# Two layers and a third part of a network on one core: three programs with barriers between them written as one

## The reference, cut to what matters

```python
for l in range(2):                                   # the two layers
    h = rms_norm(x, g_mix_pre);  u = h @ w_in        # 1024 -> 3200
    mix = concat(chunk_attention, conv_module, retention) @ w_out
    x = x + rms_norm(mix, g_mix_post)
    h = rms_norm(x, g_mlp_pre)
    f = square(relu(h @ w_up)) @ w_down              # 1024 -> 4096 -> 1024
    x = x + rms_norm(f, g_mlp_post)
# the third part
x = x + 0.5 * swiglu_ffn(rmsnorm(x, ffn1_norm))      # 1024 -> 2 x 2816 -> 1024
u = rmsnorm(x, mix_norm);  proj = u @ w_in_2
x = x + (gated sum of ssm, dilated attention, memory attention) @ w_out_2
x = x + 0.5 * swiglu_ffn(rmsnorm(x, ffn2_norm))
return rmsnorm(x, final_norm)
```

## Time and profile before

| | us |
|---|---|
| median of 3 runs | 2854.04 |
| lowest and highest | 2852.43, 2858.58 |
| the profiled execution | 2853.72 |
| its span | 2851.9 |
| PE busy | 2710.3 (95%) |
| DVE busy | 1291.4 (45%) |
| ACT busy | 1015.0 (36%) |

### The profile page before, as it was taken

How to read it: one execution, slowest core, us unless ns; L and a number is a source line. 1 busy time by engine, 2 the same in 40 slices (tenths; PEclk the granted TensorE clock), 3 DMA queues, 4 the chain that set the end, 5 groups by cost and what they waited for, 6 DMA issues and landing times. The chain is left out here.

```text
span 2851.9 us, 31899 instructions
## 1 busy us (share of the span) xinstructions
PE 2710.3 (95%) x12330; PEld 2122.2 (74%) x12330; DVE 1291.4 (45%) x1666; ACT 1015.0 (36%) x1433; POOL 287.8 (10%) x276
## 2 busy tenths in 40 slices
PE   7999899999799989999989999999999998899998
PEld 5875688887587568888768888777777666688886
DVE  4754442342574444233343333478773446333322
ACT  3333332232333333233333333433235453334322
POOL 0000000001000000000100000067540230000000
PEclk9999999999899989999999999999999999999999
DMA  3310122322231012322122322412131024122222
GB/s 123 126 53 30 59 82 95 104 88 74 72 122 45 30 59 88 103 89 103 59 82 96 103 92 91 168 60 74 53 132 52 30 75 162 61 101 90 94 91 80
DMA packets 41443, 241.88 MB, mean 85 GB/s; under 512 B 5232, under 2 KB 5744, under 8 KB 18416
## 3 DMA queue, kind: packets, MB, share of 16 engines
q1 hardware_dynamic: 41056, 239.25, 24.4%
q0 software_dynamic: 272, 1.05, 0.1%
HBM read 231.90 MB, written 8.39 MB: 84 GB/s over the span
## 5 line engine op out<-in xcount | busy, mean ns | idle before, releaser
L353 DVE TENSOR_TENSOR w_lo<-w_raw,w_hi 128x2048 fp32r<-128x2048 f32 (+3 forms) x219 | 464.2, 2120 | 850.4 <-ACT w_hi L344 850.2
L384 PE MATMUL gemm<-h_hi,w_hi 128*128 128x512 f32 x1936 | 777.7, 402 | 47.9 <-DVE h_lo L538 44.0
L384 PE MATMUL gemm<-h_hi,w_lo 128*128 128x512 f32 x1936 | 760.5, 393 | 0.0
L384 PE MATMUL gemm<-h_lo,w_hi 128*128 128x512 f32 x1936 | 760.5, 393 | 0.0
L344 ACT ACTIVATE w_hi<-w_raw 128x2048 fp32r<-128x2048 f32 (+3 forms) x219 | 383.5, 1751 | 257.5 <-PE gemm L384 254.3
L384 PEld LDWEIGHTS gemm<-h_hi,w_hi 128*128 128x128 f32 x1936 | 367.0, 190 | 139.0 <-issue 46.1
L384 PEld LDWEIGHTS gemm<-h_hi,w_lo 128*128 128x128 f32 x1936 | 367.2, 190 | 78.2
L384 PEld LDWEIGHTS gemm<-h_lo,w_hi 128*128 128x128 f32 x1936 | 368.1, 190 | 71.8 <-issue 1.7
L384 PE MATMUL gemm<-f_hi,w_hi 128*128 128x512 f32 x512 | 199.4, 389 | 0.0
L384 PE MATMUL gemm<-f_hi,w_lo 128*128 128x512 f32 x512 | 199.4, 389 | 0.0
L384 PE MATMUL gemm<-f_lo,w_hi 128*128 128x512 f32 x512 | 199.4, 389 | 0.0
(11 more groups left out here) (370 smaller groups left out, 3614.4 us busy)
## 6 DMA issues: line engine op xcount, KB each, us to landing
w_raw<-in_w SPq DMA_DIRECT2D x171, 1024.0 KB, 4.8
w_raw<-in_w SPq DMA_DIRECT2D x16, 768.0 KB, 4.2
w_raw<-in_w SPq DMA_DIRECT2D x16, 640.0 KB, 3.8
w_raw<-in_w SPq DMA_DIRECT2D x18, 512.0 KB, 3.7
bias_t<-in_att_bias SPq DMA_DIRECT2D x2, 1536.0 KB, 9.2
decay_t<-in_c_decay SPq DMA_DIRECT2D x2, 1536.0 KB, 8.2
x_sb<-in_x SPq DMA_DIRECT2D x4, 512.0 KB, 5.4
x_kept<-x_sb SPq DMA_DIRECT2D x1, 2048.0 KB, 11.0
```

Source lines behind the costliest of these rows:

```text
L353: dve.tensor_tensor(w_lo[:, b.slot, 0:size], w_raw[:, b.slot, 0:size], w_hi[:, b.slot, 0:size].bitcast(F32), ALU.subtract).then_inc(S["w_r ...
L384: mm = pe.matmul(dst, lhs, rhs, start=b.first and k == 0 and j == 0, stop=b.last and k == b.kt - 1 and j == 2)
```

## The change

The three blocks become one `nc.Block`. The layer's bodies are functions of the layer's number (`layer_tensor(pe, lay)` and so on), called twice in Python, so the outer loop is gone and the layer stands in the program twice. The semaphores are never cleared: a wait in layer `lay` adds what earlier layers have counted (`cnt`), and the norms are numbered through (`N0`). The pieces of all parts are numbered in one list. `load_next`, `round_next`, `rest_next`, `head_start`, `clear_counts` and the transfers of `first_gain` are gone; the gains of both layers and of the third part are loaded at the start. A block behind a border is now handled like every other, two blocks ahead.

```diff
-def number(pieces, tok_tiles=None):
+def number(*parts):
+    pieces = []
+    for part in parts:
+        for i, b in enumerate(part):
+            b.i = i
+            pieces.append(b)
...
-    plan1 = layer_pieces()
-    plan2, AT2 = third_pieces()
+    third_part, AT2 = third_pieces()
+    plan = number(*(layer_pieces() for _ in range(DEPTH)), third_part)
...
-        def round_block(act, plan, n, t=ONCE, whole=False):
-            if isinstance(t.n(n), int) and t.n(n) >= len(plan):
-                return
+        def piece_of(n, t):
+            if isinstance(t.i, int):
+                n, t = t.n(n), ONCE
+            return (plan[n], t) if n < len(plan) else (None, t)
+        def round_block(act, n, t=ONCE):
+            b, t = piece_of(n, t)
+            if b is None:
+                return
...
-        def clear_counts():
-            for s in S.values():
-                nc.gpsimd.sem_clear(s)
-            nc.all_engine_barrier()
...
-                norm_inverse(dve, 1)
-                for q in range(2):
-                    rest_next(dve, q)
-        clear_counts()
-        with nc.Fori(0, DEPTH) as layer:
-            with nc.Block() as block:
+            for n in range(2):
+                rest_block(dve, n)
...
                     norm_rooted(act, 3)
-                    round_next(act, 0, plan1)
                     norm_squares(act, 4, x_sb, sq_f, wait=(S["x_done"], KD))
                     norm_rooted(act, 4)
-                    round_next(act, 1, plan1)
...
                     post_norm_dve(dve, 3, gains["mlp_post"], KD)
-                    rest_next(dve, 0, n1)
-                    norm_inverse(dve, 4)
-                    rest_next(dve, 1, n1)
-            clear_counts()
...
-                head_start(dve)
-                pre_norm_dve(dve, 0, 0, first_gain)
+            pre_norm_dve(dve, N0 + 0, J0 + 0, gains["mix_pre"])
...
+        with nc.Block() as block:
+            @block.vector
+            def _(dve):
+                begin_vector(dve)
+                for lay in range(DEPTH):
+                    layer_vector(dve, lay, step)
+                third_vector(dve, step)
```

More of the change, by code:

```diff
@@ L214, in third_pieces @@
     ffn("ffn2")
-    tok_tiles = [MEMT if b.kind == "tok" and b.src == "w_kv" else TOKT for b in out]
-    return number(out, tok_tiles), start
+    return out, start
 def build(nc, ins, outs):
     A = ins
-    plan1 = layer_pieces()
-    plan2, AT2 = third_pieces()
+    third_part, AT2 = third_pieces()
+    plan = number(*(layer_pieces() for _ in range(DEPTH)), third_part)
+    n1 = (len(plan) - len(third_part)) // DEPTH
+    plan2 = plan[DEPTH * n1:]
     with ExitStack() as ctx:
@@ new lines, in begin_tensor, with begin_scalar, begin_vector @@
+        def begin_tensor(pe):
+            pe.wait_ge(consts_in, 32)
+            norm_total(pe, 1, out_sb)
+            pe.wait_ge(more_consts_in, 32)
+        def begin_scalar(act):
+            for k in range(0, KD, 2):
+                act.wait_ge(x_in[k // 2], 16)
+                norm_squares(act, 1, x_sb, out_sb, tiles=(k, k + 1))
+            act.wait_ge(eps_made, 2)
+            norm_rooted(act, 1)
+            for n in range(2):
+                round_block(act, n)
+        def begin_vector(dve):
+            dve.memset(eps_c[:], EPS).then_inc(eps_made, 1)
+            dve.memset(quarter[:], np.pi / 2).then_inc(eps_made, 1)
+            for n in range(2):
+                rest_block(dve, n)
@@ new lines, in layer_gpsimd @@
+        def layer_gpsimd(pool, lay):
+            cnt = counts(lay)
+            N0 = 1 + 4 * lay
+            pool.wait_ge(S["conv_inv"], cnt("conv_inv", 2))
+            for q in range(2):
+                tile = out_sb[:, 3 + q, :]
+                pool.tensor_tensor(tile, tile, conv_rs, ALU.mult).then_inc(S["ln_done"], 1)
+            pool.wait_ge(S["ln_done"], cnt("ln_done", 2))
+            pool.wait_ge(S["rg_gate"], cnt("rg_gate", PAIRS))
+            for j in range(1, PAIRS + 1):
+                tile = out_sb[:, 4 + j, :]
+                pool.wait_ge(S["ln_sq_s"], cnt("ln_sq_s", 2 + j))
+                pool.tensor_tensor(tile, tile, rg[:, j - 1, :], ALU.mult).then_inc(S["ret_gated"], 1)
+            squares_added(pool, N0 + 1, cnt("sq_added", 0), sq_f)
+            squares_added(pool, N0 + 3, cnt("sq_added", KD - 3), sq_f)
@@ L1250, in build @@
+            post_norm_dve(dve, N0 + 3, gains["mlp_post"], KD)
         g_hi = at("g_hi", [P, F2T, SEQ], F32R, FZ)
@@ L1346, in slot_of @@
             half, left = divmod(m + 1, b.tiles // 2)
-            return slot_at.get((b.n - first_q, half - 1)) if left == 0 else None
+            return slot_at.get((b.i - first_q, half - 1)) if left == 0 else None
         def residues(g, i):
@@ L1460, in _ @@
+                third_sync(sp)
+            @block.tensor
+            def _(pe):
+                begin_tensor(pe)
+                for lay in range(DEPTH):
+                    layer_tensor(pe, lay)
+                third_tensor(pe)
             @block.gpsimd
             def _(pool):
-                pool.wait_ge(S["units"], plan2[AT2["ffn1_down"]].u0)
-                pool.dma_start(mem_sb[:], A["mem"].rearrange("(k p) t -> p k t", p=P)).then_inc(S["mem_in"], 16)
-                squares_added(pool, 2, 0, x2_sq)
@@ L1751, in _ @@
+                for lay in range(DEPTH):
+                    layer_gpsimd(pool, lay)
+                third_gpsimd(pool)
             @block.scalar
             def _(act):
-                def evacuate(b, dst, func=ACT.Copy, scale=1.0, width=SEQ, m0=0):
-                    for m in range(b.tiles):
-                        act.wait_ge(S["units"], b.u0 + (m + 1 if b.kind == "feat" else m // 2 * 2 + 2))
-                        act.activation(dst(m), tile_of(b, m, width), func, scale=scale).then_inc(S["g_free"], 1)
@@ L2019, in _ @@
-                for b in plan2[AT2["w_out2"]:AT2["ffn2_up"]]:
-                    k = 2 * (b.n - AT2["w_out2"])
-                    if k:
-                        norm_squares(act, 3, x_sb, mix_sq, wait=(S["x2_done"], KD), tiles=(k - 2, k - 1))
-                    evacuate(b, lambda m: part[:, k + m, :])
-                    round_block(act, plan2, b.n + 2)
-                norm_squares(act, 3, x_sb, mix_sq, wait=(S["x2_done"], KD), tiles=(KD - 2, KD - 1))
-                norm_rooted(act, 3)
@@ L2027, in _ @@
-                split_hi(act, 3, 3, out_sb, S["normed"], 3 * KD)
-                ffn("ffn2", F2T)
-                norm_squares(act, 4, x_sb, out_sb, wait=(S["x2_done"], 2 * KD), tiles=(KD - 2, KD - 1))
-                norm_rooted(act, 4)
+                begin_scalar(act)
+                for lay in range(DEPTH):
+                    layer_scalar(act, lay)
+                third_scalar(act)
             @block.vector
```

2857 lines of the change are left out of this document (1415 added, 1442 removed).

## The result

The changed kernel takes 2840.04 us, the median of five runs (2839.23 to 2840.88), against 2854.04 for the kernel before in the same comparison: a ratio of 0.9948 (95% interval 0.9934 to 0.9963). The direction and the changed places came out as forecast; 4.5 us were won where the sum had nothing.

The account below looks back on a forecast made before the run. TensorE, busy 95% of the span, was taken as the bound, with gains only where it stands still. Gains of 2.9 us at the start, 4.0 and 1.2 at the borders made 8.1: 2845.9 us, range 2841.5 to 2850.5.

Parts of the forecast that it names:

- Start: Program start: first scaling at 26.36 us instead of 29.28, 2.9 us won, with the spread at the lower clock, 2.08 us.
- First border: Between the two layers: the next scaling comes 3.5 to 4.4 us earlier than at 734.11, taken as 4.0.
- The model place: Behind `w_out2` in the third part, already in the new order: 13.17 us from summing's start to scaling, assumed for both borders.
- Second border: Between second layer and third part: the scaling comes 0.8 to 1.6 us earlier than at 1438.36, taken as 1.2.
- Point (1): The layer's second copy in the program: instruction fetch could cost 3.8 us once or twice; taken as zero.
- Point (2): Clock level in the layers' norm spreads: either layer can gain or lose 1.8 us, taken as 2 us both ways.
- The rivals: Three alternative outcomes for the whole kernel: 2834.2 us (4 in 100), 2849.7 us (22 in 100), 2859.7 us (3 in 100).
- The first: At the borders the splits don't hold the norm back: 19.8 us gained, 2834.2 us; 4 in 100.
- The slower one: Clock stays down through each border's last norm: 6.9 us lost per border, 2859.7 us; 3 in 100.
- The range: Whole kernel: 2841.5 to 2850.5 us, including 2 us for the clock to either side; 71 in 100 for the forecast.

Follow-up runs that it names:

- late_splits: The changed kernel with each border's second rounding and split moved behind the post-norm's root and sums; 2829.45 us.
- unrolled_before: The kernel before with its loop over the two layers written out, barriers and clearing kept; 2846.93 us.
- experiment 10: The changed kernel with each border's second split behind the post-norm and the first norm's inversion ahead of the start's splits; 2826.87 us.
- idle_2: The changed kernel with two extra sums on DVE between spread and scaling at the first border alone; 2848.03 us.

## Why the prediction was wrong

- *Start*: forecast 2.9 us, came 2.85, with the spread at 2.07 us as taken (the 2.08 of the earlier trace rows). Right.
- *First border*: forecast 4.0 (3.5 to 4.4), came 4.37. The model place gave 13.17 us, measured 13.13; the stretch behind, 15.63, was nearer to the border's own 15.51 than to the 16.42 that I also averaged in. Right, and late_splits shows that the rounding and split in the norm's way make the 13.13 us out of 6.98.
- *Second border*: forecast 1.2 (0.8 to 1.6), came 1.65, just over the upper end, for the same reason: 13.13 + 15.56.
- *Point (1) of "What no row shows"*, the second copy at zero: right, as far as unrolled_before shows it.
- *Point (2)*, the failed step, a term of the sum that was mis-sized: "either layer can gain or lose this: 2 us both ways", around zero. In the traces it came to -4.53 us: -0.35 and -2.73 in the layers and -1.45 in the third part, which the term had left out. Three things were wrong with it. It counted only the two spreads behind `w_out`, while the level differed in the retention stage and in the additions and products beside those spreads too. It held only the layers, while the third part has gaps of its own. And it was centred on zero, although showed both that the second layer had drawn its low level and that the first had not; a change that moves that layer was likelier to give some of it back than to take more (this last is argued, not shown). Its size isn't fixed either: the second traces of the two kernels differ by 2758.46 - 2754.83 = 3.63 us there.
- *The rivals*: none came. The first (splits in nobody's way) is what the kernel becomes when they are moved, and gives 10.6 us more. The slower one needed the level to stay down through the 16 additions; they took 9.54 us at both borders (before: 9.54 and 9.89).
- *The range* took in 2 us for the clock. Two layers and a third part whose levels move apart from each other needed some 4 to 5 us on the lower side, down to about 2839 (2854.0 - 9.8 - 5). How far the time falls is in part luck of the draw, but not of one set of runs: the changed kernel's second set has 2840.68, outside the range too.

With the changed places at 8.87 us and the unchanged at 4.53 the sum is 13.40, the difference of the two spans. By the medians the clock's part is 14.0 - 8.9 = 5.1 us with the first set of runs of before, and 2852.79 - 2840.68 - 8.9 = 3.2 with the third.

What stays open: from which offset to which level. The traces, one of each kernel, show 2.7 us more in the second layer with 3.9 us of waiting ahead of it, and 1.8 less with a third idle sum than with two; they show no rule by which the level of a given gap could be told beforehand.

## What to carry to other kernels

Cut a trace at the points where a change ends, and compare the untouched stretches first: here a third of the gain (4.53 of 13.40 us in the traces) was no work that the change took away. The clearing of counters and the jump cost their time one for one here, where nothing ran beside them; and work moved off a border into the part before it must be looked for on the queues of the engines that the next chain needs: here the place of one rounding and split was worth 6 us twice, nearly as much as the whole change. Where one engine is busy nearly all the time and the rest of its time is short gaps, put the clock's level into the range on both sides: the same instructions spread over 8.5 us here, which is 0.15% of the span to either side of the middle.

## What the runs showed of the hardware

- The same program's granted clock and time go together: over the 13 runs of the kernel before in the first set, 2847.3 us at 0.975 and 2855.3 at 0.971, a slope of 1.5 us for each 0.001 (fitted; 1.4 to 1.6 in the other sets, where the expectation of experiment 10 had 1.7). Not expected: programs differ in how much they scatter. The changed kernel's first five runs lie within 1.7 us, idle_2's ten within 1.8, those of unrolled_before within 9.5. The Trainium skill (TensorE: Matmul & The Clock Gate, What's actually happening) says that the monitor of TensorE's activity runs freely, and so the same kernel meets the full clock after different numbers of matmuls from run to run, and that the cost of this rise is below 1% of a typical span. The runs agree in size: a kernel's fastest and slowest lie 0.05 to 0.33% apart here, where this whole change is worth 0.5%.
- The clearing of 59 semaphores takes POOL 4.1 us and that of 118 takes 8.6: 44 ns in the row of each, but 71 to 74 ns from start to start.
- TensorE's jump back to the head of the loop takes 3.8 us by its row. The Trainium skill (Runtime: NRT & Kernel Launch, Instruction fetch mechanics) says that a taken branch to a far target stalls until its instructions are fetched, while a straight program's fetches are mostly hidden. unrolled_before agrees: the border is 4.1 us shorter, and the second layer, run from its own copy, is not longer (671.11 us against 673.91).
